# RWKV powers, inverse and first join as compact 32-wide diagonal blocks on 32x32 tiles

## The reference, cut to what matters

```
def step(state, inp):
    r_t, w_t, k_t, v_t, a_t, b_t = inp
    sa = jnp.einsum('bhvk,bhk->bhv', state, a_t)
    state = (state * w_t[:, :, None, :] + sa[..., None] * b_t[:, :, None, :]
             + v_t[..., None] * k_t[:, :, None, :])
    return state, jnp.einsum('bhvk,bhk->bhv', state, r_t)
```

## Time and profile before

| what | value |
|---|---|
| median of 3 runs | 1585.71 us (1585.19 to 1587.72) |
| profiled execution, span from first to last instruction | 1584.8 us; its own time is not listed apart, the median lies 0.9 us above the span |
| PE busy, matmul records | 1536.4 us (97%), 14426 |
| PE weight loads busy, records | 1266.9 us (80%), 14426 |
| DVE, ACT, POOL busy | 894.3, 695.8, 120.5 us |
| instructions of all engines | 33484 |
| PSUM banks, heads for each q, q | 8, 4, 4 |

### The profile page before, as it was taken

How to read it: one execution, slowest core, us unless ns; L and a number is a source line. 1 busy time by engine, 2 the same in 40 slices (tenths; PEclk the granted TensorE clock), 3 DMA queues, 4 the chain that set the end, 5 groups by cost and what they waited for, 6 DMA issues and landing times.

```text
span 1584.8 us, 33484 instructions
## 1 busy us (share of the span) xinstructions
PE 1536.4 (97%) x14426; PEld 1266.9 (80%) x14426; DVE 894.3 (56%) x1651; ACT 695.8 (44%) x1268; POOL 120.5 (8%) x86
## 2 busy tenths in 40 slices
PE   7999999899999999999999999999999999999998
PEld 6787767779789797887887777888887888888887
DVE  3658364656474664842236997433346777777323
ACT  5543264563452634524234998423235333333222
POOL 0004000002240222412000000000000000000000
PEclk9999989999999999999999999999999999999999
DMA  6322303431010111206312000232342332323231
GB/s 221 108 80 81 102 32 111 149 104 37 29 55 11 54 37 30 55 11 148 80 55 79 2 2 11 84 107 83 105 158 68 105 101 85 107 80 106 72 124 71
DMA packets 110978, 124.40 MB, mean 78 GB/s; under 512 B 21320, under 2 KB 94664, under 8 KB 110448
## 3 DMA queue, kind: packets, MB, share of 16 engines
q1 hardware_dynamic: 107904, 114.85, 23.3%
q10 hardware_dynamic: 2928, 7.41, 1.3%
HBM read 118.04 MB, written 4.21 MB: 77 GB/s over the span
## 4 chain that ended last, share of the span: by engine, by line
PE 78%; DVE 13%; ACT 5%; issue 3%; POOL 0%; DMA 0%; DVEq 0%; SPq 0%; ACTq 0%; POOLq 0%
PE bank L807 74%; PE bank L817 4%; ACT arena L1487 3%; DVE arena L2098 2%; DVE arena L2095 2%; DVE weights_lo L2095 2%; DVE ff_c L2098 1%; ACT L1487 1%; DVE ff_c L2095 1%; DVE act_lo L2095 1%; DVE arena L2102 1%; ACT weights_hi L1487 1%; DVE ff_c L2103 1%; DVE arena L2270 1%; DVE act_t L2095 1%
## 5 line engine op out<-in xcount | busy, mean ns | idle before, releaser
L1487 ACT ACTIVATE arena<-bank 128x512 f32<-128x512 f32 (+3 forms) x415 | 225.3, 569 | 559.5 <-PE bank L807 532.9
L2095 DVE TENSOR_TENSOR weights_lo<-weights,weights_hi 128x1024 fp32r<-128x1024 f32 (+1 forms) x190 | 239.7, 1262 | 303.9 <-ACT weights_hi L1487 296.9
L807 PE MATMUL bank<-h_hi,weights_hi 128*128 128x512 f32 (+1 forms) x1008 | 402.4, 399 | 5.5 <-DVE weights_lo L2095 2.6
L807 PE MATMUL bank<-h_hi,weights_lo 128*128 128x512 f32 (+1 forms) x1008 | 394.0, 391 | 0.0
L807 PE MATMUL bank<-h_lo,weights_hi 128*128 128x512 f32 (+1 forms) x1008 | 394.0, 391 | 0.0
L807 PE MATMUL bank<-arena 64*64 64x64 f32 (+6 forms) x7746 | 344.7, 247 | 14.7 <-DVE arena L2098 5.9
L807 PEld LDWEIGHTS bank<-arena 64*64 64x64 f32 (+3 forms) x7746 | 281.4, 140 | 68.5 <-issue 57.5
L1487 ACT ACTIVATE weights_hi<-weights 128x1024 fp32r<-128x1024 f32 (+1 forms) x190 | 200.1, 1053 | 172.3 <-PE bank L807 169.5
L807 PEld LDWEIGHTS bank<-h_hi,weights_hi 128*128 128x128 f32 (+1 forms) x1008 | 190.0, 189 | 55.6 <-DVE weights_lo L2095 9.2
L807 PEld LDWEIGHTS bank<-h_hi,weights_lo 128*128 128x128 f32 (+1 forms) x1008 | 190.0, 188 | 40.8
L807 PEld LDWEIGHTS bank<-h_lo,weights_hi 128*128 128x128 f32 (+1 forms) x1008 | 190.3, 189 | 37.3
(11 more groups left out here) (172 smaller groups left out, 1628.7 us busy)
## 6 DMA issues: line engine op xcount, KB each, us to landing
weights<-in_w_in SPq DMA_DIRECT2D x39, 1024.0 KB, 5.4
weights<-in_ffn_up SPq DMA_DIRECT2D x22, 1024.0 KB, 5.1
weights<-in_ffn_down SPq DMA_DIRECT2D x10, 1024.0 KB, 5.1
weights<-in_w_out SPq DMA_DIRECT2D x8, 1024.0 KB, 5.1
weights<-in_w_in SPq DMA_DIRECT2D x16, 256.0 KB, 4.6
weights<-in_w_branch_rwkv SPq DMA_DIRECT2D x4, 1024.0 KB, 5.2
weights<-in_w_branch_nsa SPq DMA_DIRECT2D x4, 1024.0 KB, 5.2
weights<-in_w_in SPq DMA_DIRECT2D x5, 512.0 KB, 4.0
```

The lines of the kernel that those rows point to most:

```text
L807: return pe.matmul(o, w, x, start=first, stop=last)
L1487: return act.activation(o, i, f, **kw)
L2095: return dve.tensor_tensor(o, a, b, op)
```

## The change

The powers, the inverse of the blocks of 16 and the first join are block diagonal with blocks of 32. The change keeps only those blocks: the four 32-token blocks of a tile lie on the four groups of 32 partitions, each 32 columns wide. It

- replaces `pair_of_tiles` by `diagonal` in 24 operations (eight (c, h) pairs times four 32x32 products: 32 matmuls for 16), and evacuates 256 columns instead of 512;
- computes low with 32-row results (64 matmuls for 32; the second half of the columns is swapped for odd blocks) and adds "up", its transpose on the diagonal blocks (64 matmuls); gram no longer holds that part (192 columns a head for 256);
- makes the last join from two parts: `left_of` (16 matmuls, off-diagonal tiles) and `right_columns` (32 matmuls), with the left columns written by POOL (`left_ready`) and the right ones by DVE into invt_all, the 64-wide inverse that w uses;
- leaves x0 as two 64-wide operations, but moves x0 of g = 0 behind both pd 3, and x0 of g = 1 behind left_of;
- moves the evacuation of low (and up) from DVE to ACT, the centring of v from DVE to POOL, the sums over v ahead of the first transposed powers on DVE, and two masks to POOL.

```diff
+            def diagonal(j, g, w, x):
+
+                claim(pe, j)
+                for c, h, at_ in blocks_of(g):
+                    for p in subs:
+                        ins = mm(ps(j)[p, at_:at_ + SUB], w[p, c, h, :], x[p, c, h, :])
+                fill(j, ins)
...
+            def left_of(j, g):
+
+                claim(pe, j)
+                for c, h, at_ in blocks_of(g):
+                    for p in (1, 3):
+                        ins = mm(ps(j)[subs[p - 1], at_:at_ + SUB], low_left[subs[p], c, h, :], invt[subs[p], c, h, :])
+                fill(j, ins)
+
+            def right_columns(j, g):
+
+                claim(pe, j)
+                for c, h, at_ in blocks_of(g):
+                    for n, p in enumerate(subs):
+                        if n % 2:
+                            ins = mm(ps(j)[p, at_:at_ + SUB], ident[p, p], invt[p, c, h, :])
+                        else:
+                            ins = mm(ps(j)[p, at_:at_ + SUB], inv[p, c, h, :], mid[p, c, h, :])
                 fill(j, ins)
...
-                        for x in range(2):
-                            for z in both:
-                                tok = slice(c * P + z.start, c * P + z.stop)
-                                ins = mm(ps(J[q, "low", x])[z, at_:at_ + DH], a_r[both[x], n, c, 0, z], b_h[both[x], n, tok])
...
+                        for m, p in enumerate(subs):
+                            for x in range(2):
+                                z = slice(c * P + DH * (m // 2), c * P + DH * (m // 2) + DH)
+                                keys = b_h[both[x], n, z]
+                                if m % 2:
+                                    keys = keys.rearrange("p (k t) -> p k t", k=2)[:, ::-1, :]
+                                ins = mm(ps(J[q, "low", x])[p, at_:at_ + DH], a_r[both[x], n, c, 0, p], keys)
...
+                                ins = mm(ps(J[q, "up", x])[p, at_:at_ + SUB], b_h[both[x], n, tok], a_r[both[x], n, c, 0, p])
...
-                    pair_of_tiles(J[q, "pa", g, 0], g, ba, pw_even)
-                    pair_of_tiles(J[q, "pb", g, 0], g, pw_even, ba)
+                    diagonal(J[q, "pa", g, 0], g, ba, pw_even)
+                    diagonal(J[q, "pb", g, 0], g, pw_even, ba)
...
+                pair_of_tiles(J[q, "x0", 0], 0, ka, v_by_head)
                 for g in range(2):
...
+                    left_of(J[q, "mu", g, 1], g)
+                pair_of_tiles(J[q, "x0", 1], 1, ka, v_by_head)
...
+                    right_columns(J[q, "my", g, 1], g)
...
             def to_pair(j, g, o):
-                copy_out(j, o[:, 2 * g:2 * g + 2].rearrange("p c h x -> p (c h x)"))
+                copy_out(j, o[:, 2 * g:2 * g + 2].rearrange("p c h x -> p (c h x)"), width=256)
```

More of the change, by code:

```diff
@@ L60 @@
 CHUNK = 64
+SUB = 32
 ARENA = 43200
@@ L239, in build_program @@
         at += 48
-        gram = view(at, TT, 4, 256)
-        pw_even, invt, inv, mid = (view(at + 4096 + 1024 * n, TT, 4, DH) for n in range(4))
+        gram = view(at, TT, 4, 192)
+        ba, pw_even, join, invt, inv, mid = (view(at + 3072 + 512 * n, TT, 4, SUB) for n in range(6))
         pw_odd, pwt = inv, mid
+        invt_all = view(at + 6144, TT, 4, DH)
         m_all, s_all, s_part = (view(at + 4096 + 1024 * n, 2, 2, TT, DH) for n in (0, 2, 3))
         s_all = s_all.rearrange("p a b c v -> p (a b c v)").rearrange("p (m n v) -> p m n v", n=2, v=DH)
-        ba, br, ka, kr = (gram[:, :, :, n * DH:(n + 1) * DH] for n in range(4))
+        br, ka, kr = (gram[:, :, :, n * DH:(n + 1) * DH] for n in range(3))
         r_q, k_q, v_q, lw_q, b_q, pm_q, pi_q, pp_q, av_q, kk_q, t1_q, t2_q = (
@@ L421, in build_program @@
             job(q, "v", 1)
-            twice(q, "tb", "tk", "low")
+            twice(q, "tb", "tk", "low", "up")
             for c in range(TT):
@@ L1216, in _ @@
                     wait_read(pe, J[q, "pd", g, 2])
-                    pair_of_tiles(J[q, "pd", g, 3], g, pw_odd, invt)
-                    pair_of_tiles(J[q, "x0", g], g, ka, v_by_head)
+                    diagonal(J[q, "pd", g, 3], g, pw_odd, invt)
+                pe.wait_ge(sem("v_centred"), q + 1)
+                for c in range(TT):
+                    for x in range(2):
+                        wait_read(pe, J[q, "gram", c, x])
+                pair_of_tiles(J[q, "x0", 0], 0, ka, v_by_head)
                 for g in range(2):
@@ L1246, in _ @@
                     if c % 2 == 0:
+                        pe.wait_ge(sem("left_ready"), 2 * q + c // 2 + 1)
                         wait_read(pe, J[q, "my", c // 2, 1])
@@ L1748, in to_pair, with by_parity @@
             def to_pair(j, g, o):
-                copy_out(j, o[:, 2 * g:2 * g + 2].rearrange("p c h x -> p (c h x)"))
+                copy_out(j, o[:, 2 * g:2 * g + 2].rearrange("p c h x -> p (c h x)"), width=256)
+            def by_parity(j, o, x, n):
+                wait_full(act, j)
+                read(j, run(o[:, :, x:4:2, :], ps(j)[:, 0:8 * n].rearrange("p (c n s) -> p c n s", c=TT, n=2), ACT.Copy))
             def rwkv_out(q):
@@ L1810, in _ @@
                 for kind, dst in (("tb", b_tok), ("tk", k_tok), ("tv", v_tok)):
+                    if kind == "tv":
+                        for x in range(2):
+                            by_parity(J[q, "low", x], low, x, DH)
+                        for x in range(2):
+                            by_parity(J[q, "up", x], ba, x, SUB)
                     for n in range(2):
@@ L2508, in _ @@
                 mix_of(q, "v", 1)
-                for x in range(2):
-                    j = J[q, "low", x]
-                    wait_full(dve, j)
-                    read(j, tt(low[:, :, x:4:2, :], ps(j).rearrange("p (c n s) -> p c n s", c=TT, n=2),
-                               m_low.unsqueeze(1).unsqueeze(1).broadcast_to([P, TT, 2, DH]), ALU.mult))
                 for c in range(TT):
@@ L2518, in _ @@
                         wait_full(dve, j)
-                        read(j, tt(gram[:, c, x:4:2, :], ps(j).rearrange("p (n s) -> p n s", n=2), over(m_gram, 2),
+                        read(j, tt(gram[:, c, x:4:2, :], ps(j)[:, 0:384].rearrange("p (n s) -> p n s", n=2), over(m_gram, 2),
                                    ALU.mult))
@@ L2535, in _ @@
                 then(dve.reduce_sum(stat[:, 36:52], by_16(v_tok), axis=AX.X))
-                then(ts(stat[:, 36:52], stat[:, 36:52], -1.0 / DH))
+                ts(stat[:, 36:52], stat[:, 36:52], -1.0 / DH).then_inc(sem("v_means"), 1)
+                for g in range(2):
+                    transposed_power(g, 0)
                 for g in range(2):
@@ L2548, in _ @@
                     sum_into(J[q, "pd", g, 3], g, invt)
+                stream_to(next_k)
                 for g in range(2):
```

132 lines of the change are left out of this document (71 added, 61 removed).

## The result

The changed kernel takes 1695.39 us (median of 4 runs, 1692.51 to 1696.45) where the kernel before took 1585.45 us (1583.12 to 1587.72): a ratio of 1.0684, 95% interval 1.067 to 1.0697, so it is slower by nearly 7%. Forecast were 1698 us and a range of 1655 to 1735.

What follows compares the result with a forecast made beforehand. PE was taken as the bound, busy 97%, its program arriving only just in time in the powers stage. Supply 95, behind w 4 and clock 13 make +112 us on a span of 1584.8: 1698 us, range 1655 to 1735.

Steps and rivals of the forecast that it cites:

- Supply binds at 3.65 us a block: From low to w, PE's program arrives in 256-instruction blocks, one on the way, 3.65 us each; chance 0.84.
- three late starts and two counts divisible by 256: Earlier trace: PE resumed late at 465.21, 489.88 and 701.34; 1536 and 10496 instructions lie between, 6 and 41 blocks.
- Low to w 61.4 us: First low to first w product: 0.9 + 16.4 x 3.65 + 0.6 = 61.4 us, against 37.6 before.
- the 23.8 of the sum: Low to w would take 23.8 us more in each of four quarters, +95 us in all.
- 1.1 to 1.3 us from request to packet: Delay from PE entering a block to the next block's packet; packet to usable 2.4 to 2.5 us more.
- Behind w 4 us and the clock 13 us: Blocks without lead behind w cost 1 us a q, +4; half clock for w and perhaps e's start 3.3, +13.
- A diagonal operation in 0.47 to 0.55 us, a block run off in 1.0: PE's own time for 64 records of 32x32 tiles, and for one block of 256 instructions.
- the floor rival: A small product costs as much as a 64-wide one, 0.93 us an operation; without supply trouble 1594 us; chance 0.04.
- PE idle two thirds of the stage: Sign in the changed profile, low to w: PE idle two thirds, cause "issue", in stretches of over 2 us.
- Copies and moves cost nothing: Smaller evacuations and work moved to ACT and POOL lie under PE's operations and wait: 0 us.
- The fast rival, 1541: Supply does not bind, small tiles pay: powers stage 18.3 us for 29.5, 45 us less, 1541 us; chance 0.08.

Runs made afterwards that it cites:

- b_split: The kernel before, with each 64x64 product of powers, joins and x0 issued as two products of 32 result rows, same results: 1682.16 us, ratio 1.0602.
- a_fourth: The changed kernel, its diagonal and turning operations computing only two of eight (c, h) blocks, the rest copied (values wrong): 1570.38 us, ratio 0.9902 to the kernel before.
- a_lump: The changed kernel with 22 extra wide products a quarter, overwritten, all ahead of the first diagonal operation of the powers: 1775.26 us, ratio 1.1187 to the kernel before.
- a_centre_dve: The changed kernel with v centred on DVE again, behind the first sums, instead of on POOL: 1699.84 us, ratio 1.071 to the kernel before.
- a_filled: The changed kernel with one extra wide product, overwritten, ahead of each of 22 diagonal operations a quarter: 1703.05 us, ratio 1.0725 to the kernel before.
- a_v_spread: The changed kernel with half the v projection moved into the powers, three records at a time, its transposes behind level 1: 1711.14 us, ratio 1.0786 to the kernel before.

## Why the prediction was right, step by step

- **Supply binds at 3.65 us a block.** Right, and shown: eleven blocks in 40.2 us, 147 packets as forecast. It rested on three late starts and two counts divisible by 256. The first of these starts was of another kind than I took it for: weights streamed at up to 392 GB/s until its packet came. b_split shows that the number of instructions is sufficient as a cause, a_fourth that the rest of the change costs nothing to speak of, a_lump that the lead is one block.
- **Low to w 61.4 us.** Measured 61.7 in q = 0 and 63.8 in the mean, 26.2 more than before for the 23.8 of the sum: the term was 2.4 us a q too small, 10 us in all. From the powers to w the four q take 48.6 to 49.7 us; from low to the powers they take 12.6, 16.6, 15.5 and 13.9. So the spread lies in the front. I took 1.1 to 1.3 us from request to packet everywhere; in the front, where weights stream, it was 1.7 to 2.8. By my estimate that is 1.2 us a q in the mean, half of the error. The other half stays open: I counted tv and bonus by their instructions alone, they are long products with few instructions, and a_lump shows that only one block is fetched behind such a run. That this is the rest is argued; the front wasn't tried alone.
- **Behind w 4 us and the clock 13 us.** Measured 4.6 together, so this term was mis-sized by 12 us. The clock did fall, to 0.63 to 0.70 in the mean from low to w, but in the window behind w it was 0.96 in q = 0, 0.83 in q = 1 (the one that took 2.7 us longer than before) and 0.99 in q = 2. I had read from the earlier trace rows that a starved stage hands on a low clock; here it mostly doesn't. The two errors nearly cancel, and 1698 for 1695 looks better than the terms are.
- **A diagonal operation in 0.47 to 0.55 us, a block run off in 1.0.** Slightly low: 0.57 and 1.1 at the full clock. That refutes the floor rival (0.93 us); that such a difference hides under the supply was forecast rightly.
- **PE idle two thirds of the stage.** Wrong: 36% (23 of 64 us). At the lower clock a burst takes 1.93 us. The prediction had about 2 us for that itself, but reckoned the idle share with the 1.2 of the full clock; the longer busy time cost nothing. The gaps were mostly 1.3 to 2.5 us, not all over 2.
- **Copies and moves cost nothing.** Right as far as tried (a_centre_dve); DVE and ACT waited for PE.
- **The fast rival, 1541.** Its reckoning of PE's own time was sound: 8.9 ns records are there. It fell on the program's arrival: 3.65 us a block, where any gain at all needed under 2.2.

## What to carry to other kernels

Before splitting a product into smaller tiles, count PE's instructions of the stage, weight loads and waits included, in blocks of 256: in the unrolled dense stretches here they started 3.5 to 3.65 us apart, and each packet more cost 3.0 to 3.6 us. A stage already at that pace gets slower with the instructions added, however short. Long products belong between the short ones (a_filled, two to a block, 92 us for 8), not in one lump, since PE's program comes only one block ahead; that was shown with extra products, and moving real ones in gained nothing in three tries. Before work is moved, ask which wait it covers at its old place, at what clock it will run at the new one, and which load of weights moves with it: a block asked for while weights streamed came 1.7 to 2.9 us after PE had entered the one before, where 1.2 was usual.

## What the runs showed that I had not expected

- Four 32x32 tiles in turn run fp32 records at 8.9 ns each at the full clock, against 14.6 ns for 64x64 ones: 0.6 of the time for half the columns and half the weights.
- 22 wide products in one place or in 22 places differ by 72 us, at 149 packets each.
- A starved PE may keep 2.4 GHz (b_split, 1.00 with PE busy 17.8 of 28 us) or run much of its stage at 1.2 (the changed kernel, 0.63 in the mean with 30.5 busy of 49.1 us from the powers to w of q = 0, 0.50 in single bursts); in both the blocks were 3.5 to 3.65 us apart.
- PE's program shares the DMA engines with the weights: behind a piece of weights (99% of the engines' time) the packet of a block started 2.8 us after PE had entered the block before, and the gap grew to 3.86 us, in the changed kernel and in a_v_spread alike.
